# Another order of page sums, state steps and low parts in a one-core decoder step

## What is computed

```python
proj = rms_norm(h, g_pre) @ w_in                 # q (512), k (512), v (1024), g (1024) and a low-rank gate gk
b = cumsum(log_sigmoid(gk) / 16)                 # per chunk of 64 tokens, 4 heads of 128
S_c = exp(b_last) * S_{c-1} + (k * exp(b_last - b)).T @ v     # 8 chunks: the state steps
o = (q * exp(b)) @ S + causal((q * exp(b)) @ (k * exp(-b)).T) @ v
h = h + (rms_norm(o) * silu(g)) @ w_out          # output projection
h = h + sigmoid(rms_norm(h) @ w_gate) * (p @ w_up)            # embedding gate
k_new, v_new = rms_norm(h) @ w_kv                # shared keys and values
q1, g1 = rms_norm(h) @ w_in1                     # second layer: queries and second gate
z = q1 . K / sqrt(64) + bias                     # samples: over 16 pages of 128 cached keys each
```

## Time and profile before

| | us |
|---|---|
| median of the runs | 899.49 |
| profiled execution | 896.14 |
| its span, first to last instruction | 894.4 |
| TensorE busy | 854.3 (96%) |
| VectorE busy | 545.4 (61%) |
| ScalarE busy | 455.6 (51%) |
| GpSimd busy | 277.9 (31%) |
| mean granted TensorE clock | 0.992 |

### The profile page before, as it was taken

The page is one execution under the profiler, slowest core; times in us unless marked ns, Lnnn a source line. Parts: engine busy times, 40 slices in busy tenths (PEclk is TensorE's granted clock), DMA queues, the critical chain, the costliest instruction groups (busy, mean ns, idle before and its releaser), DMA issues.

```text
span 894.4 us, 14835 instructions
## 1 busy us (share of the span) xinstructions
PE 854.3 (96%) x5069; PEld 594.5 (66%) x5069; DVE 545.4 (61%) x670; ACT 455.6 (51%) x1532; POOL 277.9 (31%) x149
## 2 busy tenths in 40 slices
PE   5999999999999999999989999999989999999995
PEld 3566667767754444444578877878744554899995
DVE  4545375598847779988993722222267767553553
ACT  5511482237648686778763411212377666534433
POOL 3000000956766998977760000000100000021110
PEclk9999999999999999999999999999999999999998
DMA  9799868656699988979984079989898889221202
GB/s 332 276 373 400 320 227 289 203 178 210 206 318 377 370 307 313 353 272 370 374 298 160 1 265 342 357 309 308 295 341 291 298 295 341 95 95 48 95 1 96
DMA packets 109435, 232.52 MB, mean 260 GB/s; under 512 B 7473, under 2 KB 66552, under 8 KB 109360
## 3 DMA queue, kind: packets, MB, share of 16 engines
q1 hardware_dynamic: 50864, 171.67, 52.9%
q10 hardware_dynamic: 58496, 59.90, 20.1%
HBM read 220.41 MB, written 11.14 MB: 259 GB/s over the span
## 4 chain that ended last, share of the span: by engine, by line
PE 73%; DVE 9%; DMA 5%; issue 5%; ACT 4%; POOL 1%; SPq 1%; ACTq 0%; POOLq 0%; DVEq 0%
PE pp L1618 19%; PE pp L1605 14%; PE pp L1621 9%; PE pp L2037 6%; PE pp L1994 4%; DVE slot L1285 3%; PE pp L2021 2%; PE pp L1582 2%; PE pp L1602 2%; DMA w_raw<-in_gla_w_in_dram 2%; PE pp L2008 2%; PE pp L1633 2%; POOL slot L616 1%; DMA slot<-in_cache_k_dram 1%; PE pp L1698 1%
## 5 line engine op out<-in xcount | busy, mean ns | idle before, releaser
L616 POOL TENSOR_TENSOR slot<-slot,qb 128x1024 f32<-128x1024 f32 x95 | 246.4, 2623 | 101.1 <-DMA slot<-in_cache_k_dram 62.6
L1286 DVE TENSOR_REDUCE zall<-slot 128x16 f32<-128x1024 f32 x99 | 119.1, 1215 | 22.7 <-POOL slot L616 21.6
L1101 DVE TENSOR_TENSOR w_lo<-w_raw,w_hi 128x1024 fp32r<-128x1024 f32 x57 | 78.5, 1378 | 75.9 <-ACT w_hi L666 75.9
L822 ACT ACTIVATE slot<-slot 128x64 f32<-128x64 f32 x464 | 111.0, 241 | 22.3 <-POOL slot L616 22.2
L666 ACT CAST w_hi<-w_raw 128x1024 fp32r<-128x1024 f32 x58 | 60.5, 1045 | 77.1 <-PE pp L1621 39.4
L822 ACT ACTIVATION_READ_ACCUMULATOR slot<-slot 128x1 f32 x464 | 87.1, 188 | 0.0
L1605 PE MATMUL pp<-xn,w_raw 128*128 128x512 f32 x192 | 84.3, 593 | 0.5 <-ACT xn L677 0.5
L1605 PE MATMUL pp<-xn,w_unsplit 128*128 128x512 f32 x192 | 83.9, 592 | 0.0
L1621 PE MATMUL pp<-xa_hi,w_hi 128*128 128x512 f32 x200 | 81.7, 408 | 1.6 <-DVE w_lo L1101 1.6
L1621 PE MATMUL pp<-xa_hi,w_lo 128*128 128x512 f32 x200 | 79.0, 395 | 0.0
L1618 PE MATMUL pp<-xb_hi,w_hi 128*128 128x260 f32 x384 | 78.8, 286 | 0.2 <-DVE w_lo_k L1101 0.2
(11 more groups left out here) (305 smaller groups left out, 1437.9 us busy)
## 6 DMA issues: line engine op xcount, KB each, us to landing
slot<-in_cache_k_dram SPq DMA_DIRECT2D x128, 512.0 KB, 5.9
slot<-in_cache_v_dram SPq DMA_DIRECT2D x120, 512.0 KB, 5.6
w_raw<-in_gla_w_in_dram ACTq DMA_DIRECT2D x12, 1024.0 KB, 8.5
slot<-in_gla_w_in_dram SPq DMA_DIRECT2D x24, 512.0 KB, 10.0
w_raw<-in_w_kv_dram ACTq DMA_DIRECT2D x8, 1024.0 KB, 10.1
w_raw<-in_w_ple_gate_dram ACTq DMA_DIRECT2D x6, 1024.0 KB, 5.3
s<-in_state_gla_dram SPq DMA_DIRECT2D x1, 4096.0 KB, 26.8
out_dram<-s ACTq DMA_DIRECT2D x4, 1024.0 KB, 11.0
```

The source lines that it names most:

```text
L616: nc.gpsimd.tensor_tensor(slot[s][:], slot[s][:], qb[:, (n // NPG) % 2, :], ALU.mult).then_inc(S("k_mul_pool"), 1)
L822: ins = nc.scalar.activation(part, part, ACT.Copy, accum_out=zall[:, n % NPG, b * SH + h:b * SH + h + 1])
L1101: nc.vector.tensor_tensor(lo, raw, hi.bitcast(F32), ALU.subtract).then_inc(S("w_split"), 1)
L1286: nc.vector.tensor_reduce(zall[:, n % NPG, b * SH:(b + 1) * SH], at.rearrange("p (h d) -> p h d", d=HD), AX.X, ALU.add).then_inc(S("k_used ...
```

## The change

- `PAGES_AT`: in the value stage the jobs have 0, 0, 0, 0, 2, 3, 3, 2 pages instead of 0, 0, 0, 0, 1, 3, 2, 2; the first two tiles of the output projection have five instead of four; the second gate has none instead of four. So `FEW` is 30 instead of 28.
- ScalarE copies the value rows ahead of the decay exponentials.
- VectorE makes the low part of gate tile 1 at u = 7 of the value stage, ahead of that step's page sums, instead of at the start of the gate stage, behind them.
- In odd gate steps VectorE does all eight state steps in one piece, ahead of `gate_normed` and of the pages. In even ones from u = 2 the order stays.

```diff
--- before.py
+++ after.py
@@ -65,8 +65,8 @@
 
 
 PAGES_AT = {}
-for _name, _c in (("v", (0, 0, 0, 0, 1, 3, 2, 2)), ("g", (2, 3, 2, 3, 2, 3, 2, 3)), ("wo0", (4,) * 8), ("ple0", (4,) * 8),
-                  ("q1", (4,) * 8), ("g1", (4, 0, 0, 0, 0, 0, 0, 0))):
+for _name, _c in (("v", (0, 0, 0, 0, 2, 3, 3, 2)), ("g", (2, 3, 2, 3, 2, 3, 2, 3)), ("wo0", (5, 5, 4, 4, 4, 4, 4, 4)), ("ple0", (4,) * 8),
+                  ("q1", (4,) * 8)):
     for _u in range(PHASES[_name][1]):
         PAGES_AT[PHASES[_name][0] + _u] = _c[_u]
 PAGES_THROUGH = {}
@@ -832,10 +832,10 @@
             for u in range(1, 8):
                 if u < 7:
                     split_hi(PHASES["v"][0] + u + 2)
+                v_rows(u - 1)
                 if u < 3:
                     decays_exp(2 * u - 2)
                     decays_exp(2 * u - 1)
-                v_rows(u - 1)
 
             def o_copies(h):
 
@@ -1291,8 +1291,7 @@
                 if u >= 2:
                     dve.wait_ge(S("v_t"), u - 1)
                 normed(j, work[:, 2 + u % 2, :])
-                if u < 7:
-                    split_lo(j + 2)
+                split_lo(j + 2)
                 if u == 1:
                     decays_sum(3)
                 if u in (1, 2):
@@ -1345,16 +1344,16 @@
             for u in range(8):
                 h = u // 2
                 j = PHASES["g"][0] + u
-                if u % 2 == 0:
-                    split_lo(j + 1)
-                gate_normed(j)
                 if u % 2:
-                    state_steps(h, range(4))
+                    state_steps(h, range(NCH))
+                    gate_normed(j)
                     if h < GH - 1:
                         score_pages(j, 0, 2)
-                    state_steps(h, range(4, NCH))
                     gate_silu(j, u)
                 else:
+                    if u:
+                        split_lo(j + 1)
+                    gate_normed(j)
                     if h >= 2:
                         gate_o(h - 2)
                     if h:
```

## The result

The changed kernel took 900.71 us (median, 898.16 to 905.6), the kernel before, beside it on the same chip, 897.58 us (894.28 to 901.68): a ratio of 1.0032, 95% interval 1.0019 to 1.0046. That is 0.3% slower, where 0.4% faster was predicted. The profiled execution took 898.76 us, with a span of 897.0.

The account below looks back on a forecast made before the run. TensorE was taken as the bound, so only its waits could give time. The terms -1.0 + 3.5 - 6.2 = -3.7 took the median 899.49 to 895.8 us, in a range from 888.5 to 901.5.

Parts of the forecast that it names:

- The bound: Whole kernel: TensorE, busy 854.3 of 894.4 us, is the bound, so only its idle places can give time back.
- Part 5: Second gate without pages: the 3.4 us wait for tile 1 and the clock loss go, -6.2 us, margin 0.3 us.
- Part 1: Value rows copied ahead of decays: the 1.21 us wait goes; gain 1.0 us, bounds 0.2 and 1.21.
- a wait for q1 rows under 1 us: Sign expected in the new profile after the value copy's move: TensorE's wait for q1 weight rows stays below 1 us.
- Part 2: Value stage, more pages: low part's 1.39 us wait goes; new 4.0 us wait before head 0's state products, 2.8 us half speed.
- my 1.0 shift: Everything after the value copy's move was taken to stand 1.0 us earlier than in the old trace.
- Part 3: Gate stage, state steps in one piece: they hide, but the output of head 0 begins 3.5 us later.
- the cover: Gate stage: odd gate tiles normalised 4 us or more later cost nothing; 1 to 2 us if cover goes.
- Part 4: Output projection, two pages more in its first two steps: cost 0, bound +0.6 us, no wait there.
- 1.8 us of cover for at most 2.4 us of delay: Output projection: tile 7's square ready by 318.3, wanted at 320.06, against the delay from VectorE's extra product.
- the second gate's wait stays: Rival: VectorE's lag grows by over 3 us, dropping pages there brings 0 to 3; 900.5 us, chance 0.18.
- The slower one: Rival: GpSimd bounds the value stage, its eighth product ending at 181 or later; 905 us, chance 0.09.

Follow-up runs that it names:

- order_only: The changed kernel with the old table of pages, so only the new order of instructions against the kernel before; 894.91 us, ratio 0.9968.
- the last run above: New order, old pages, spread page sums, plus the gate's product of heads 0 and 1 one step earlier; 890.63 us, ratio 0.9914 to the kernel before.
- half_loads: The changed kernel, but pages 38 to 63 load only one half, 256 KB instead of 512; ratio 1.0011 to the kernel before.
- late_five: The changed kernel with its two five-page jobs at tiles 4 and 5 of the output projection instead of 0 and 1; 904.62 us, ratio 1.0067.
- pages_only: The kernel before with the new table of pages and the old order of instructions; 902.65 us, ratio 1.0055.

## Why the prediction was wrong

**The bound and Part 5: right.** The second gate's wait went and the clock stayed at 1.00: 6.66 us against 6.2. VectorE's last page products took 1.22 us, as forecast. Its tile 1 was normalised at 470.7, and TensorE, 8.25 us late, would have asked for it near 472.65, so the margin was 1.9 us and not 0.3: the delays ahead helped it. What the wait costs is shown by another edit too: spreading the sums gave 0.53% (0.33 to 0.73), some 4.7 us.

**Part 1: right in kind, half in size.** The value copy's wait is gone; the q1 rows' waits grew from 0.61 to 1.44 in two. The run had started 0.64 us late (98.36 for 97.72 at the same wait), which makes the gain 0.5 us, in the bounds of 0.2 to 1.2. The transfers did not move along fully, and of the sign "a wait for q1 rows under 1 us" only the single waits (0.80 and 0.64) keep to it.

**Part 2: right.** GpSimd's eighth product was forecast for 178.1, its sum for 179.3, the copy for 184.4, less 1.0. Measured: the sum ends at 179.24, the copy at 184.21, and TensorE waits 4.08 us, where 4.0 was forecast. Here my 1.0 shift was not there, since Part 1 gave less and the run began late. The half speed cost 2.0 us instead of 2.8: from 184.35 to the output of head 0 it is 9.87 us, where the same work at full clock needs 7.86 (10.06 before, less its wait of 1.94 and of 0.26).

**Part 3: the steps right, the cover wrong by a little.** The output of head 0 begins without a wait, 2.3 us later, where 3.5 less 1.0 was forecast. That it began at 194.22 with 194.3 forecast is in part luck, two errors that cancel: 0.9 us of Part 1's shift was missing, and the half speed cost 0.8 less. But what I called covered, the odd gate tiles' later normalising, was not: at 218.05 TensorE idles 0.81 us for the gate's product of head 0, queued on VectorE behind gate tile 3's silu and a low part, and 0.75 us are lost by 269. I had priced that at 1 to 2 if the cover went. `order_only` has such waits, of 1.72 and 0.49 us, there in the new order alone, and with the product one step earlier (the last run above) the first of them is gone.

**Part 4: the step that failed.** I wrote "Cost 0, bound +0.6", and it was 5.1 us. The working had two premises. One, the ring "turns two pages later, so that page 30 needs page 28 summed, near 253", looked at the front of the ring only. It did not follow it to the first page of the third tile, which with five pages a tile stands behind two pages of the tile before that wait for their slots, in a queue with a query load ahead and on DMA engines that were already full. The other, "1.8 us of cover for at most 2.4 us of delay", took one VectorE product as the delay. GpSimd in truth starts 6.7 us later in TensorE's time; less 1.8 that is 4.9, and measured is 5.1. That this comes out is in part luck: by the same sum `half_loads` and the query's later load would wait 2.3 and 2.4 us, and both together 0.3, where 3.0, 3.0 and 1.6 were seen, so the cover is no fixed 1.8. And `late_five` shows that even without a late start the work itself is no "cost 0": one product and sum more for VectorE made its step 1.8 to 3.3 us longer. That GpSimd does not catch up is in its row before, 24 products in one run: VectorE's residuals then come 7.93 us apart, and TensorE's two waits too (320.28, 328.21).

**The sum.** Forecast -1.0 + 3.5 + 0 - 6.2 = -3.7. Measured -0.5 (0.6 late at the start, 0.1 at 142) and, from that 0.1 on, +2.3 + 0.75 + 5.1 - 6.66 = +1.5, so +1.6 at 479 and +2.6 at the end; the medians differ by 3.1. With Part 4 at its true price the forecast would have been +1.4. The measured 900.71 us lies inside the stated range of 888.5 to 901.5, but that range held a gain as well as a loss, so this speaks for none of the working.

**The rivals.** None of the mechanisms named came about. The time fell where "the second gate's wait stays" had put it (900.5), by another cause, so it bears out nothing of that rival. The slower one, GpSimd as the bound, had the right engine in the wrong stage: I weighed it in the value stage, where it has 10 products, and not from the projection on, where it has 24 in one run.

## What to carry to other kernels

When work is moved into a stage, follow the ring and the load queue through to the first item of each later step, and count what stands ahead of it in the queue: eight slots are two tiles of four, but not two of five, so that two pages and a query came before the third tile's first. A row of one engine that says "24 in one run" is a warning: here most of a late start was still there at the end of the stage, and giving work to VectorE instead did not help. And before a short wait is cured by moving work elsewhere, try the engine's order in place: halving the batches ahead of the late instruction gave 0.5%; moving its pages away, and others with them, cost 0.55%.

## What the hardware showed

The clock did not fall by the length of a wait. After 1.94 us of idle before the output of head 0 it stayed full; the kernel before with only the second gate's sums spread has the same wait, 1.93 us, and the clock was 0.61 from 192 to 196. The eight products took 3.08 us instead of the 1.99 of the earlier trace rows:

```profile
192.13 3.08 PE L1868 MATMUL pp<-vtok,attT 128*128 128x256 f32 x8 [1.93 <-DVE states L1320]
```

In the projection 2.92 us left it full in the changed kernel (clock 1.00 from 316 to 328), and 2.30 us brought 0.57 in `pages_only`. The Trainium skill (TensorE: Matmul & The Clock Gate, Part 1: The HAM clock gate) says that how many matmuls run slowly at a kernel's start differs from run to run. It speaks of the start; these rows show a like spread for one wait in the middle, with the loss and without it. Where the clock fell the loss was 1.1 us (3.08 for 1.99) at head 0, 1.8 (8.94 for 7.18) and 2.8 (9.99 for 7.18) at the second gate, and 2.0 behind the new wait for attT.

What stays open: the 2 us of GpSimd's lateness that the other two steps leave were not taken apart; why the waits follow its start by two thirds only; and that the embedding gate takes two extra pages at 1.56 us, but four at 5.97. For the last, VectorE's longer products beside GpSimd's (3.38 and 2.85 us) were seen, but not tested as the cause.
